# RWKV chain: block inverse of the first half four places later in its slot, group norm of a tile in the next first-half slot

## The chip, the cores and the metric

One NeuronCore of a Trainium2 chip. The metric is the device time of one launch in microseconds (us). Before the change three runs took 3611.99, 3619.16 and 3623.68 us, median 3619.16.

## What is computed

A backbone of four layers over 256 context and 256 latent tokens, width 1024, fp32. Layers 0 and 3 mix tokens with a bidirectional RWKV-7 delta rule, layer 1 with Mamba-2, layer 2 with windowed attention; a gated ConvFFN follows each. The change touches the RWKV mixer alone:

```python
def step(s, inp):                       # one token of one direction, state s (64 x 64) of each of 16 heads
    r_t, w_t, k_t, v_t, kk_t, a_t = inp
    s_kk = einsum('bhvk,bhk->bhv', s, kk_t)
    s = s * w_t - s_kk (kk_t * a_t) + v_t k_t
    return s, einsum('bhvk,bhk->bhv', s, r_t)
...
y = head_groupnorm(ys[0] + ys[1], ln_g, ln_b) + bonus     # bonus: per head, times v
y = (y * (sigmoid(xg @ g1) @ g2)) @ wo
```

## The kernel before

The kernel is written engine by engine: TensorE (PE), VectorE (DVE), ScalarE (ACT), GpSimd (POOL) and SyncE (SP) each run their own program and meet at semaphores. The RWKV mixer first projects (r, k, v and three low-rank inputs), then works through eight tiles of 128 channels (two heads each). A tile has 512 tokens in eight chunks of 64, for each of two directions. Within a chunk the recurrence is written with the inverse of a 64 x 64 triangular matrix; from chunk to chunk it is a chain.

`slot_steps` (L2384) sets one order that all engines follow, each taking the steps it has code for. Seventeen slots, numbered h from 0: slot 2i, an **even slot**, prepares the first half (four chunks) of tile i, slot 2i+1, an **odd slot**, its second half. In each slot the chain runs over four chunks of the half prepared in the slot before. A chain chunk is six places: W, U, S, each for two directions, so a slot has places 0 to 23. The other steps stand in two lists, `early` (ahead of the chain step of that place) and `late` (behind it). A step on an engine waits at its turn, and what stands behind it on that engine waits too. The steps spoken of:

- **W, U, S**: chain. PE multiplies into PSUM; ACT copies W's result (L2835), DVE copies U's (L3194), and S ends with the new state on DVE (L3205), for which ACT scales the old one (L2930). S writes no state in the last chunk of a tile, which is the last of an even slot.
- **GT**: PE forms the matrices to invert, ACT copies them. SP sends them to DRAM and back with another layout (L2499, L2507), POOL inverts 16 x 16 blocks in **IB** (L3003 to L3009), SP sends the result out and back (L2514, L2522), and DVE spreads it in **E** (`expand`: two products L3158, two transposes L3162, L3163). GT of a first half stands at places 0, 1 of an odd slot, GT of a second half at 19, 20. E of a second half is at place 2 of an odd slot.
- **Z, X**: two levels (16, 32) that grow the block inverse to 64: four Z and four X on PE per half, of 16 matmuls each, with copies on ACT (Z) and DVE (X, L3185, and a transpose L3190).
- **H2, HB, R**: products of keys; H2 uses PSUM bank 6, and DVE masks its result (L3177).
- **L01, L23, KS, ...**: staging of tile i+1 in the even slot: low-rank products, two sigmoids each on ACT (L2846), scans on DVE (L3084) with L3088, L3092, L3097 behind, and **ar0**, **ar1**, the last operations, on POOL (L2997, L2998); ar1 follows the last chain step of the even slot.
- **P1, P2, P2e, P2v, P3**: group norm of a finished tile. P2 is a 128x512 matmul of variances into bank 6 on PE, then a logarithm (L2946) on ACT; P2e the exponential (L2950) on ACT; P2v two products on DVE (L3213, L3215); P3 the gate's matmul into bank 6 and on DVE the output of the tile (L3220). They stand at places 18 to 22 of the odd slot after the tile's chain has ended. YE copies a tile's chain output out of PSUM at an even slot's end.

In layer 3 only the latent half of the tokens is wanted behind the chain, so its group norm works on 256 columns in place of 512.

Of the kernel before, what the change touches and what calls it, by code (L numbers as in the profile page):

```python
# [134 lines left out]
def program(nc, a, out, draft, scratch, blocks_dram, layers=range(DEPTH), mixers=True, only=range(DEPTH)):  # L135
    C = Counts(draft)
    ctx = ExitStack()
    with ctx:
# [38 lines left out]
        vec_done = sem("vec_done")  # L177
# [2206 lines left out]
        def slot_steps(h):  # L2384

            i, s = h // 2, h % 2
            chain = [(k, 2 * ((h - 1) // 2) + d, 4 * ((h - 1) % 2) + c) for c in range(4) for k in "WUS" for d in range(2)]
            chain = chain if h else []
            if h == SLOTS:

                steps = []
                for n, step in enumerate(chain):
                    steps.append(step)
                    if n % 2:
                        steps.append(("O", n // 12, n // 2 % 6, n // 2 % 6 + 1))
                return steps + [("YE", i - 1), ("O", 2, 0, 3), ("P1", i - 1), ("O", 2, 3, 6), ("P2", i - 1)] + [
                    ("O", m, 6, 7) for m in range(3)] + [("P2e", i - 1), ("O", 3, 0, 4), ("P2v", i - 1), ("P3", i - 1),
                                                         ("O", 3, 4, 7)]
            both = (2 * i, 2 * i + 1)
            more = i + 1 < KD  # L2400
            levels = [(k, q, s, m) for m in range(len(LEVELS)) for k in "ZX" for q in both]
            early, late = [], []
            if s == 0:
                at = (4, 5, 7, 8, 10, 11, 13, 14) if i else (21, 21, 22, 22, 23, 23, 24, 24)
                early += [(k, *step) for k, step in zip(at, levels)]
                early += [(1 if i else 20, "E", i, 0), (0, "R", i, 0, 0), (2, "R", i, 0, 1), (9, "H2", both[0], 0),
                          (12, "HB", both[0], 0, 0), (15, "HB", both[0], 0, 1), (16, "H2", both[1], 0),
                          (18, "HB", both[1], 0, 0), (20, "HB", both[1], 0, 1)]
                late.append((3, "Rv", i, 0))
                if i == 0:  # L2410
                    early += [(0, "IB0", 0, 0), (0, "IB", 0, 1), (0, "kf", 1), (0, "TS", 1)]
                else:
                    late.append((3, "IB", i, 1))
                if more:
                    late += [(k, n, i + 1) for k, n in (
                        (1, "L01"), (2, "sc0"), (3, "L23"), (3, "sub0"), (3, "sc1"), (4, "TL"), (4, "sub1"),
                        (5, "sum1"), (6, "KS"), (7, "KE"), (8, "pn0"), (9, "pr0"), (9, "pn1"), (11, "rm0"), (12, "ax0"),
                        (13, "ax1"), (14, "ar0"), (15, "ad0"))]
            else:
                at = (5, 6, 8, 9, 12, 13, 15, 16)  # L2420
                early += [(k, *step) for k, step in zip(at, levels)]
                early += [(2, "E", i, 1), (14, "R", i, 1, 0), (17, "R", i, 1, 1), (2, "H2", both[0], 1),
                          (3, "HB", both[0], 1, 0), (4, "HB", both[0], 1, 1), (7, "H2", both[1], 1),
                          (10, "HB", both[1], 1, 0), (11, "HB", both[1], 1, 1)]
                late.append((18, "Rv", i, 1))
                if more:
                    early += [(d, "GT", i + 1, 0, d) for d in range(2)] + [(19 + d, "GT", i + 1, 1, d) for d in range(2)]
                    late += [(1, "ar1", i + 1), (8, "IB", i + 1, 0)]
                    late += [(k, n, i + 1) for k, n in (
                        (3, "pct"), (4, "rm1"), (6, "pr1a"), (7, "ad1"), (8, "pr2a"), (12, "pr1b"), (13, "pr2b"), (14, "bsum"),  # L2430
                        (14, "bs"), (16, "BV"), (16, "BVv"), (19, "sd0"), (19, "sd1"), (13, "VT"))]
                if i + 2 < KD:
                    late += [(23, "kf", i + 2), (23, "TS", i + 2)]
                if i:
                    late += [(k, n, i - 1) for k, n in ((4, "P1"), (18, "P2"), (18, "P2e"), (21, "P2v"), (22, "P3"))]
            steps = []
            for k in range(25):
                steps += [e[1:] for e in early if e[0] == k]
                if k < len(chain):
                    steps.append(chain[k])  # L2440
                steps += [b[1:] for b in late if b[0] == k]
            if s == 0 and i:
                steps.append(("YE", i - 1))
            return steps
# [100 lines left out]
        def rwkv_pe(l, lo):  # L2545
            t = f"r{l}"
# [67 lines left out]
            def grams_k(q, s):  # L2614
                i, d = q // 2, q % 2
                if d:
                    pe.wait_ge(vec_done, C.at(f"{t}.{q - 1}.g2{s}"))
                elif s:
                    pe.wait_ge(vec_done, C.at(f"{t}.{q + 1}.g20"))
                elif i + 1 < KD:  # L2620
                    pe.wait_ge(act_done, C.at(f"{t}.t{i + 1}.kkl"))
                else:
                    pe.wait_ge(vec_done, C.at(f"{t}.t{i - 2}.out"))
                pe.wait_ge(vec_done, C.at(f"{t}.t{i}.sd{d}"))
                ar = AR[i % 2]
                for c in range(4):
                    cs = tok(ORDER_Q[d][4 * s + c])
                    for hs in HALF:
                        if lo and s == 0:
                            last = mm(PS[hs, 6, c * P:c * P + Q], SD[hs, d, cs], ar[hs, d, 0, cs])  # L2630
                        else:
                            last = mm(PS[hs, 6, c * P:c * P + P], SD[hs, d, cs], ar[hs, d, :, cs])
                done(last, f"{q}.h2{s}")
# [106 lines left out]

            def post2(j):
                if j + 2 < KD:
                    pe.wait_ge(vec_done, C.at(f"{t}.t{j + 2}.bv"))
                elif j + 1 < KD:
                    pe.wait_ge(vec_done, C.at(f"{t}.{2 * j + 3}.g21"))
                else:
                    pe.wait_ge(vec_done, C.at(f"{t}.t{j - 1}.out"))
                pe.wait_ge(act_done, C.at(f"{t}.t{j}.sq"))
                done(mm(PS[:, 6, lo:T], const("blkmean"), SQ[:, lo:T]), f"t{j}.va")
# [26 lines left out]
            def l01(n):  # L2776
                if n:
                    pe.wait_ge(act_done, C.at(f"{t}.t{n - 1}.vt"))
                    pe.wait_ge(vec_done, C.at(f"{t}.t{n - 3}.out" if n >= 3 else f"{t}.t{n - 1}.bv"))
                for d in range(2):  # L2780
                    low_rank(n, W2A, TH, d, 6 + d, f"t{n}.pw{d}")

# [611 lines left out]
```

## Time and profile before

| what | value |
|---|---|
| median of three runs | 3619.16 us |
| profiled execution, its own time | 3610.41 us |
| its span | 3608.6 us |
| PE busy over the span | 3447.1 us, 96% |
| DVE, ACT, POOL busy | 69%, 32%, 16% |
| chain, layer 0, 283.8 to 643 us | 359.2 us, PE busy 323.67, granted clock 0.98 |
| chain, layer 3, 2985 to 3342 us | 357.0 us, PE busy 306.68, granted clock 0.98 |

The first rows are of the whole launch, the last two of the stretches in which the seventeen slots run. DVE, ACT and POOL are busy for 222.78, 191.00 and 170.21 us of the first of these. A matmul of 64 columns lasts 218 ns by its record while the next ones follow at a pace of 29 ns, so PE counts as busy in part of a stall.

### The profile page before, as it was taken

The numbers are of one execution on the slowest core, as the hardware profiler recorded it, in microseconds if no ns is written. First come the engines' busy times: TensorE is split into PE (matmuls) and PEld (weight loads), VectorE is DVE, ScalarE is ACT, GpSimd is POOL, SyncE is SP. The second block draws the span as 40 slices with busy tenths as digits, with TensorE's granted clock in tenths as the row PEclk, the third lists the DMA queues.
The fourth block names the chain that finished last, engine by engine and source line by source line (L and its number), as shares of the span: only waits on it lengthen the run. The fifth ranks groups of instructions, "written<-read, shape, count | busy, mean of one in ns | idle before, by whom it ended". The sixth has DMA issues, their size and how long they took to land. (4 is left out here: it accounts for less than half of the span.)

```text
span 3608.6 us, 74335 instructions
## 1 busy us (share of the span) xinstructions
PE 3447.1 (96%) x28653; PEld 2513.5 (70%) x28653; DVE 2487.9 (69%) x4562; ACT 1156.4 (32%) x2482; POOL 590.4 (16%) x1128
## 2 busy tenths in 40 slices
PE   7998998999999999999999999999999997888999
PEld 2447777688786455555888876678877456777887
DVE  7986665489897657653898954469987956664431
ACT  4035554133202444431233014323310225663210
POOL 1015553000000323320000000000000105553000
PEclk9998999999999999999999999999999998999999
DMA  6641111244353323223444520043434541111454
GB/s 219 207 136 24 21 22 32 74 133 130 118 161 97 105 79 102 82 76 99 129 126 127 162 83 28 25 126 121 136 118 129 170 129 25 25 24 27 134 152 133
DMA packets 584315, 365.07 MB, mean 101 GB/s; under 512 B 126144, under 2 KB 553480, under 8 KB 581928
## 3 DMA queue, kind: packets, MB, share of 16 engines
q1 hardware_dynamic: 557544, 250.40, 25.1%
q0 software_dynamic: 26432, 110.07, 8.7%
q8 instruction: 223, 3.65, 0.4%
q14 instruction: 116, 0.95, 0.1%
HBM read 348.73 MB, written 11.67 MB: 100 GB/s over the span
## 5 line engine op out<-in xcount | busy, mean ns | idle before, releaser
L275 PE MATMUL PS<-H,WR 128*128 128x512 f32 (+1 forms) x1424 | 477.1, 494 | 0.0
L591 DVE SCALAR_TENSOR_TENSOR WORK<-WORK,SC 128x512 f32<-128x512 f32 x616 | 418.3, 746 | 0.7
L275 PEld LDWEIGHTS PS<-H,WR 128*128 128x128 f32 x1424 | 268.0, 190 | 187.3 <-issue 167.2
L2549 PE MATMUL PS<-WORK 64*64 64x64 f32 (+2 forms) x6944 | 361.0, 231 | 29.5 <-ACT BIG L2846 16.6
L571 POOL DMA_DIRECT2D WORK<-in_ada_w_dram x88 | 66.4, 755 | 1857.7 <-DVE WORK L591 839.6
L1474 PE MATMUL PS<-BIG,WR 128*128 128x512 f32 (+1 forms) x944 | 329.4, 503 | 5.2 <-DMA WR<-in_rw_wo_dram 1.7
L2549 PEld LDWEIGHTS PS<-WORK 64*64 64x64 f32 (+1 forms) x6944 | 282.1, 139 | 69.2 <-ACT WORK L2835 23.0
L1474 PEld LDWEIGHTS PS<-BIG,WR 128*128 128x128 f32 x944 | 175.7, 190 | 132.6 <-issue 111.8
L2835 ACT ACTIVATE WORK<-PS 128x64 f32<-128x64 f32 (+3 forms) x528 | 161.4, 326 | 292.0 <-PE PS L2549 286.7
L1012 ACT ACTIVATE WORK<-PS 128x512 f32<-128x512 f32 x252 | 134.7, 541 | 335.6 <-PE PS L945 285.1
L945 PE MATMUL PS<-BIG 128*128 128x256 f32 x984 | 223.9, 380 | 0.0
L275 PE MATMUL PS<-WORK,WR 128*128 128x512 f32 (+1 forms) x544 | 211.7, 545 | 0.9 <-DMA WR<-in_rw_wr_dram 0.9
L945 PEld LDWEIGHTS PS<-BIG 128*128 128x128 f32 x984 | 186.0, 190 | 25.1
L2549 PE MATMUL PS<-BIG,WORK 64*64 64x64 f32 x1920 | 145.7, 228 | 47.0 <-DVE WORK L3194 36.3
L945 PE MATMUL PS<-H,BIG 128*128 128x256 f32 x768 | 177.8, 380 | 0.6 <-ACT H L728 0.4
L945 PE MATMUL PS<-BIG,WORK 128*128 128x256 f32 x792 | 176.3, 379 | 0.0
L1093 DVE SCALAR_TENSOR_TENSOR WORK<-WORK,PV 128x510 f32<-128x510 f32 x252 | 171.7, 743 | 2.6 <-ACT WORK L1023 2.6
L275 PEld LDWEIGHTS PS<-WORK,WR 128*128 128x128 f32 x544 | 102.0, 190 | 101.0 <-issue 88.5
L945 PEld LDWEIGHTS PS<-BIG,WORK 128*128 128x128 f32 x792 | 150.5, 190 | 20.5
L945 PEld LDWEIGHTS PS<-H,BIG 128*128 128x128 f32 x768 | 145.2, 190 | 22.5 <-ACT H L728 3.0
L3009 POOL TENSOR_TENSOR BTN<-BTN,BTP 64x14 f32<-64x14 f32 (+1 forms) x420 | 149.8, 357 | 32.9
L2549 PEld LDWEIGHTS PS<-BIG,WORK 64*64 64x64 f32 x1920 | 100.6, 136 | 74.0 <-DVE WORK L3194 23.4
(363 smaller groups left out, 6391.0 us busy)
## 6 DMA issues: line engine op xcount, KB each, us to landing
WORK<-in_ada_w_dram POOLq DMA_DIRECT2D x88, 1024.0 KB, 6.3
WR<-in_ffn_w_in_dram SPq DMA_DIRECT2D x220, 256.0 KB, 2.9
BIG<-in_ffn_w_in_dram SPq DMA_DIRECT2D x132, 256.0 KB, 3.4
WR<-in_ffn_w_out_dram SPq DMA_DIRECT2D x106, 256.0 KB, 2.8
WR<-in_ssd_w_in_dram SPq DMA_DIRECT2D x96, 256.0 KB, 2.8
BIG<-scratch_dram POOLq DMA_DIRECT2D x8, 2048.0 KB, 7.9
BIG<-in_ffn_w_out_dram SPq DMA_DIRECT2D x36, 256.0 KB, 3.2
BIG<-in_ada_w_dram SPq DMA_DIRECT2D x4, 2048.0 KB, 15.5
```

Source lines behind the costliest of these rows:

```text
L275: mm = pe.matmul(outs, WR[:, slot, k, 0:m], rhs(k), start=first and k == 0, stop=last and k == nk - 1)
L571: pool.dma_start(AW[:, 2048 * h:2048 * h + 2048].rearrange("p (k c) -> p k c", k=4), rows(a["ada_w"][l])[:, 4 * h:4 * h + 4, n * 512:n * 5 ...
L591: lag(vec.scalar_tensor_tensor(ACC3[:, s_], w, by, ACC3[:, s_], ALU.mult, ALU.add), label)
L945: mm = pe.matmul(out, lhs(k), rhs(k), start=start and k == 0, stop=stop and k == 3)
L1012: s(act.activation(EV[f % 2][:, n0:n0 + n, :], ps[:, 0:n, :], ACT.Copy), lab(f, "e" + bank))
L1093: lag(vec.scalar_tensor_tensor(dst, whole[h][:, :, t // 2:SEG - 1 + t // 2], tap(t, h, f), dst, ALU.mult, ALU.add), lab(f, "cv") if (t, h) ...
L1474: mm = pe.matmul(PS[:, bank, lo:T], WR[:, opened[label], k, :], rhs(8 * r + k), start=r == 0 and k == 0, stop=last and k == nk - 1)
L2549: return pe.matmul(o, lhs, rhs, start=start, stop=stop)
L2835: s(act.activation(dst, src, ACT.Copy), f"{t}.{label}")
L3009: g(pool.tensor_tensor(below, below, product, ALU.add), f"{t}.t{i}.ib{s_}" if j_ == BLK - 2 else None)
```

## The change

```diff
@@ slot_steps, even slots (s == 0) @@
-                at = (4, 5, 7, 8, 10, 11, 13, 14) if i else (21, 21, 22, 22, 23, 23, 24, 24)
+                at = (8, 9, 11, 12, 14, 15, 17, 18) if i else (21, 21, 22, 22, 23, 23, 24, 24)
                 early += [(k, *step) for k, step in zip(at, levels)]
-                early += [(1 if i else 20, "E", i, 0), (0, "R", i, 0, 0), (2, "R", i, 0, 1), (9, "H2", both[0], 0),
+                early += [(5 if i else 20, "E", i, 0), (0, "R", i, 0, 0), (2, "R", i, 0, 1), (9, "H2", both[0], 0),
...
+                if i >= 2:
+                    late += [(k, n, i - 2) for k, n in ((18, "P2"), (18, "P2e"), (21, "P2v"), (22, "P3"))]
@@ slot_steps, odd slots @@
-                    late += [(k, n, i - 1) for k, n in ((4, "P1"), (18, "P2"), (18, "P2e"), (21, "P2v"), (22, "P3"))]
+                    late.append((4, "P1", i - 1))
+                if not more:
+                    late += [(k, n, i - 1) for k, n in ((18, "P2"), (18, "P2e"), (21, "P2v"), (22, "P3"))]
@@ PE, grams_k (H2): what frees PSUM bank 6 @@
-                    pe.wait_ge(vec_done, C.at(f"{t}.{q + 1}.g20"))
+                    pe.wait_ge(vec_done, C.at(f"{t}.t{i - 2}.out" if i >= 2 else f"{t}.{q + 1}.g20"))
...
-                    pe.wait_ge(vec_done, C.at(f"{t}.t{i - 2}.out"))
+                    pe.wait_ge(vec_done, C.at(f"{t}.t{i}.bv"))
@@ PE, post2 (P2) @@
-                    pe.wait_ge(vec_done, C.at(f"{t}.t{j + 2}.bv"))
+                    pe.wait_ge(vec_done, C.at(f"{t}.{2 * j + 5}.g20"))
@@ PE, l01 (L01) @@
-                    pe.wait_ge(vec_done, C.at(f"{t}.t{n - 3}.out" if n >= 3 else f"{t}.t{n - 1}.bv"))
+                    pe.wait_ge(vec_done, C.at(f"{t}.t{n - 1}.bv"))
```

The levels Z and X and the step E of the first half move four places back in every even slot but the first. P2 to P3 of tiles 0 to 5 move from odd slots 3, 5, ..., 13 to even slots 4, 6, ..., 14; tiles 6 and 7 keep theirs. Nothing is added or left out, and no shape changes. The waits on bank 6 follow the new order.

DVE at the start of an even slot (the names of buffers are those of the profile; L3205 and, changed, L3209 are the new chain state of S; line numbers of the changed kernel are four higher). Before:

```order
L3158 TENSOR_TENSOR WORK<-WORK,K 128x256 x2
L3162 STREAM_TRANSPOSE WORK<-WORK 128x256
L3163 STREAM_TRANSPOSE WORK<-WORK 128x256
L3194 COPY WORK<-PS 128x64
L3084 SCALAR_TENSOR_TENSOR BIG<-WORK,BIG 128x512
L3194 COPY WORK<-PS 128x64
L3170 TENSOR_TENSOR WORK<-PS,K 128x2x256
L3088 TENSOR_TENSOR BIG<-BIG 128x512
L3084 SCALAR_TENSOR_TENSOR BIG<-WORK,BIG 128x512
L3205 SCALAR_TENSOR_TENSOR WORK<-PS,WORK 128x64
L3092 TENSOR_TENSOR BIG<-BIG 128x512
L3205 SCALAR_TENSOR_TENSOR WORK<-PS,WORK 128x64
```

And changed:

```order
L3198 COPY WORK<-PS 128x64
L3088 SCALAR_TENSOR_TENSOR BIG<-WORK,BIG 128x512
L3198 COPY WORK<-PS 128x64
L3174 TENSOR_TENSOR WORK<-PS,K 128x2x256
L3092 TENSOR_TENSOR BIG<-BIG 128x512
L3088 SCALAR_TENSOR_TENSOR BIG<-WORK,BIG 128x512
L3209 SCALAR_TENSOR_TENSOR WORK<-PS,WORK 128x64
L3096 TENSOR_TENSOR BIG<-BIG 128x512
L3162 TENSOR_TENSOR WORK<-WORK,K 128x256 x2
L3166 STREAM_TRANSPOSE WORK<-WORK 128x256
L3167 STREAM_TRANSPOSE WORK<-WORK 128x256
L3209 SCALAR_TENSOR_TENSOR WORK<-PS,WORK 128x64
```

The four instructions of E stood first; now they stand between the two states of the slot's first chain chunk.

PE at the end of an even slot, changed (64x64 and 64x32 rows are HB, W, U and S; 128x512 rows are P2 and P3):

```order
L2553 MATMUL PS<-K,BIG 64x64 x8
L2553 MATMUL PS<-BIG,WORK 64x64 x2
L2553 MATMUL PS<-WORK,H 64x64 x2
L2553 MATMUL PS<-WORK,K 128x512
L2553 MATMUL PS<-BIG,WORK 64x64 x2
L2553 MATMUL PS<-WORK,H 64x64 x2
L2553 MATMUL PS<-K,BIG 64x64 x8
L2553 MATMUL PS<-WORK 64x64 x4
L2553 MATMUL PS<-WORK,BIG 64x64 x2
L2553 MATMUL PS<-WORK 64x64 x2
L2553 MATMUL PS<-H,WORK 64x64 x2
L2553 MATMUL PS<-WORK 128x512
```

Both 128x512 rows are new here; P2 stands between the two W of the last chunk, P3 between its two S.

DVE at the same place, changed, running into the odd slot:

```order
L3198 COPY WORK<-PS 128x64 x2
L3217 TENSOR_TENSOR WORK<-WORK 128x512
L3219 SCALAR_TENSOR_TENSOR WORK<-WORK,PV,BIG 128x512
L3224 SCALAR_TENSOR_TENSOR BIG<-WORK,PV,PS 128x512
L3162 TENSOR_TENSOR WORK<-WORK,K 128x256 x2
L3166 STREAM_TRANSPOSE WORK<-WORK 128x256
L3167 STREAM_TRANSPOSE WORK<-WORK 128x256
L3181 TENSOR_TENSOR WORK<-PS,K 128x512
L3198 COPY WORK<-PS 128x64 x2
```

The rows of P2v and P3 (L3217, L3219, L3224) are new between the last two copies of U and E of the second half.

## Rows read from the trace of the kernel before

**Rows 1.** Stretches: odd slot 9, even slot 10 (start:end, length, then busy us by engine, granted clock, DMA):
```profile
478.40:503.00 24.60, 22.43 (x562) 18.45 (x562) 15.90 (x41) 12.17 (x32) 9.39 (x29) 1.00 0.16 25
503.00:525.50 22.50, 19.99 (x542) 17.90 (x542) 16.07 (x36) 15.60 (x37) 16.14 (x33) 1.00 0.11 21
```
**Rows 2.** Waits of PE, 283 to 605 us, then 2975 to 3345 us (total, times, longest):
```profile
PE PS L2549 <- DVE WORK L3194: 15.6, 20, 1.9
...
PE PS L2549 <- DVE WORK L3194: 24.9, 30, 2.1
```
**Rows 3.** Timeline, PE and DVE where slot 10 becomes slot 11 (start, busy, [idle before <-releaser]):
```profile
522.00 2.09 DVE L3158 TENSOR_TENSOR WORK<-WORK,K 128x256 f32<-128x256 f32 x2 [1.89 <-DMA WORK<-blocks_dram]
525.82 0.33 PE L2549 MATMUL PS<-BIG,WORK 64*64 64x64 f32 x4 [1.67 <-DVE WORK L3194]
```
**Rows 4.** Timeline, SP's issues for tile 5:
```profile
495.41 0.37 SPq L2522 DMA_DIRECT2D WORK<-blocks_dram  x1
497.41 1.26 SPq L2499 DMA_DIRECT2D blocks_dram<-WORK  x2
...
519.61 0.37 SPq L2522 DMA_DIRECT2D WORK<-blocks_dram  x1
```
**Rows 5.** Timeline, POOL at that boundary (ar1):
```profile
521.13 1.27 POOL L2997 TENSOR_TENSOR H<-BIG 128x512 f32<-128x512 f32 x1 [1.35 <-PE PS L2549]
522.49 1.33 POOL L2998 TENSOR_TENSOR H<-BIG,WORK 128x512 f32<-128x512 f32 x1
```
**Rows 6.** Timeline, DVE, step E at the start of slot 13:
```profile
567.79 0.76 DVE L3158 TENSOR_TENSOR WORK<-WORK,K 128x256 f32<-128x256 f32 x2 [0.54 <-PE PS L2549]
568.66 0.45 DVE L3162 STREAM_TRANSPOSE WORK<-WORK 128x256 f32<-128x256 f32 x1
569.03 0.40 DVE L3163 STREAM_TRANSPOSE WORK<-WORK 128x256 f32<-128x256 f32 x1
```
**Rows 7.** Timeline, PE, end of slot 9 (P2, then waits):
```profile
494.02 1.12 PE L2549 MATMUL PS<-WORK,K 128*128 128x512 f32 x2
...
497.10 0.33 PE L2549 MATMUL PS<-WORK 64*64 64x64 f32 x4 [0.52 <-ACT WORK L2835]
...
500.21 0.28 PE L2549 MATMUL PS<-WORK,H 64*64 64x64 f32 x4
500.63 0.33 PE L2549 MATMUL PS<-BIG,WORK 64*64 64x64 f32 x4
```
**Rows 8.** Timeline, ACT, the same place:
```profile
495.25 0.69 ACT L2946 ACTIVATE WORK<-PS,MC 128x512 f32<-128x512 f32 x1 [0.82 <-PE PS L2549]
496.03 0.63 ACT L2950 ACTIVATE WORK<-WORK 128x512 f32<-128x512 f32 x1
```
**Rows 9.** Timeline, PE, end of slot 15 (P2 there has no GT behind it):
```profile
630.93 0.33 PE L2549 MATMUL PS<-WORK 64*64 64x64 f32 x4 [1.18 <-ACT WORK L2835]
```
**Rows 10.** Timeline, PE, start of slot 10 (L23 and a Z; an X; W):
```profile
503.67 1.74 PE L2549 MATMUL PS<-WORK 64*128 64x512 f32 x20 [0.68 <-ACT BIG L2846]
...
508.71 0.66 PE L2549 MATMUL PS<-WORK 64*64 64x32 f32 x16
509.20 0.31 PE L2549 MATMUL PS<-BIG,WORK 64*64 64x64 f32 x4
```
**Rows 11.** Timeline, DVE, the same place:
```profile
506.98 0.25 DVE L3205 SCALAR_TENSOR_TENSOR WORK<-PS,WORK 128x64 f32<-128x64 f32 x1
507.33 0.69 DVE L3092 TENSOR_TENSOR BIG<-BIG 128x512 f32<-128x512 f32 x1
```
**Rows 12.** Timeline, DVE, E of tile 1's first half, layers 0 and 3:
```profile
313.32 0.76 DVE L3158 TENSOR_TENSOR WORK<-WORK,K 128x256 f32<-128x256 f32 x2 [4.73 <-DMA WORK<-blocks_dram]
...
3025.50 0.76 DVE L3158 TENSOR_TENSOR WORK<-WORK,K 128x256 f32<-128x256 f32 x2 [2.99 <-DMA WORK<-blocks_dram]
```
**Rows 13.** Timeline, DVE, E at the start of slot 15, layer 0:
```profile
612.87 0.76 DVE L3158 TENSOR_TENSOR WORK<-WORK,K 128x256 f32<-128x256 f32 x2 [3.98 <-DMA WORK<-blocks_dram]
```
**Rows 14.** Timeline, PE, P2 in layer 3:
```profile
3191.66 0.70 PE L2549 MATMUL PS<-WORK,K 128*128 128x256 f32 x2
```

## The prediction

> **What bounds the kernel now.** The page first: PE is busy for 96% of the launch, and only the two chains, 359 and 357 us, hold stalls that a new order can move. Then the stretches of two slots [rows 1]: an odd slot takes 24.6 us with 22.43 of PE busy, an even one 22.5 with 19.99. PE comes first, with about 2 us of idle time per slot; DVE and ACT have room on the whole (16 us each at most), but they run in order, so what counts is who stands behind whom. Then PE's waits [rows 2]: by far the largest is for the copy of U (L3194), 15.6 us in layer 0 and 24.9 in layer 3. The timeline says where [rows 3]: at the start of the odd slot DVE stands at E of the second half, whose transfer lands at 522.00; PE resumes 3.8 us later, 1.67 us of it idle. So behind PE lies a **round trip**: from the issue of the grams at 497.41 [rows 4], through POOL's block inverse, to E at 522.00, 24.6 us, most of which no engine's order shortens. In layer 0 it begins once GT of the second half is copied (495.41 is the issue before it, so SP had been free since 495.8).
>
> **Part 1: the group norm leaves the odd slot.** P2 fills PE from 494.02 to 495.08 by its successor's start, 1.06 us, and P3 has its shape: 2.1 us. In its wake PE idles 0.52 us for a copy on ACT that stands behind the logarithm and the exponential [rows 7, 8], and 0.3 us at 500.63, where the new state waits behind the norm's products on DVE (500.21 to 500.63 less a pace of 0.12). The odd slot gets 2.9 us shorter. P2 also stands ahead of GT, so the grams could leave some 1.4 us earlier: 1.06 of PE and 0.3 of the queue on ACT; but SP is free only at 495.8, so 1.6 us is the most.
>
> **Part 2: it enters the even slot.** The same 2.1 us of PE, and no longer the delayed state, since the last chunk of a tile writes none. The copy behind logarithm and exponential stays: in slot 15, where no GT fills PE meanwhile, it costs 1.18 us [rows 9]; here the 16 matmuls of an HB fill some 0.47, so I take 0.8, between 0.52 and 1.18. The even slot gets 2.9 us longer. Parts 1 and 2 cancel, 0 per pair of slots, with ends of -0.3 and +0.4.
>
> **Part 3: the levels move back.** An X takes 0.49 us (508.71 to 509.20), and between L23 at 503.67 and the second W at 509.20 PE now does two Z and one X: 1.4 us [rows 10]. That is filler: the chain there waits for the staging's sigmoids on ACT and the scans on DVE. DVE finishes the first new state at 507.23 and the subtraction L3092 at 508.02 [rows 11]; with E behind it (0.76 and two transposes, until 1.64 us after its start [rows 6]) and the state of 0.28, it would finish at 509.9, or 0.5 earlier because L01 no longer stands behind the norm's output. So the W of 509.20 comes at 509.4, although 1.4 us of work has been taken from ahead of it: PE loses about 1.5 us here. Later the levels fill small stalls: the slot has some 0.6 us of them behind the first chunk (22.50 less 19.99 is 2.5 idle, 1.67 of it at E). Net **+0.9 us** per even slot, between 0 (the chain gets by without filler) and +1.6.
>
> **Part 4: where E and the round trip end.** A pair of slots can't go faster than half of round trip plus rest, since the grams of one tile leave before the inverse of the last is used. With 1.6 us less of round trip and 0.9 more of rest, a pair in layer 0 changes by (-1.6 + 0.9)/2, -0.35. Against this stands DVE at the boundary: P3's output, 0.75 us, now stands right ahead of E, so that even a landed inverse is spread only while ar1 runs on POOL from 521.13 to 523.82 [rows 5]. The rows show what that costs: E's two products took 2.09 us at 522.00, of which the second ended only behind ar1, against 0.76 at 567.79, when POOL was quiet [rows 3, 6]. The 1.67 us of idle time would then stay, and come back in the two layer 0 pairs that lack it now (0.54 of waiting at E in slot 13, and PE not idle). I put this between 0 and +1.9 per pair and take +0.8: a pair in layer 0 changes by +0.5, five of them by **+2.5**.
>
> **Part 5: the first tiles, layer 3, the end.** E of tile 1's first half waits 4.73 us in layer 0 and 2.99 in layer 3 [rows 12]. Four places later, about 4 us of PE's work, nearly all of that is covered; but E of its second half is bound by its own round trip, so half of some 3 and 2 us remains, less a starved start: -1 each, **-2**. In layer 3 P2 and P3 take 0.6 us each for 256 columns [rows 14], logarithm and exponential less, E meets ar1 already, and its round trip isn't begun by GT (the issues follow each other), so it doesn't shorten: -0.2 to +0.9 per pair, I take 0. Slot 14, which gets the norm without any staging, has 3.98 us of waiting at E of the last half behind it [rows 13], which cover the 2.9; what slot 13 saves is lost there too.
>
> **Sum.** +2.5 - 2 + 0 = +0.5 us against the profiled execution's 3610.4. That execution lies 8.8 us below the median of the three runs, 3619.2, so the forecast is **3619 us** for the median: no change. A measurement of this kernel can tell about 0.3%, 11 us, from none.
>
> **Rivals.**
> 1. *Covered after all, faster: 3602 us, chance 0.17.* The chain gets through the even slot's start without the filler (part 3 at 0), the 0.8 us of part 2 is covered by the levels that now stand late, and with the shorter round trip E's idle time vanishes: ten pairs gain 1.67 less 0.2 each, 15 us, and tile 1 gives 2. For it: PE has work at all places of an even slot from 2 to 18. Against it: DVE's queue [rows 11].
> 2. *Starved start, slower: 3633 us, chance 0.23.* PE has nothing beside L01, L23 and KS, and the state behind E is late, for 1.6 us in each of the twelve even slots (2 to 12, two layers) that have levels and staging, with nothing given back later: 19 us, less 2 for tile 1 and 3 for the round trip of layer 0. It decides once PE reaches the slot's second W more than 0.9 us ahead of the state. For it: the 0.68 us of idle time ahead of 503.67 [rows 10] is such a wait already. Against it: in layer 3 DVE has no mask of R at that place.
> 3. *The round trip hides everything: 3617 us, chance 0.12.* E lands when it lands; odd slots get shorter and the idle time at E longer by the same amount, and only tile 1's 2 us remain.
> 4. *E beside ar1 in full: 3625 us, chance 0.15.* Part 4 at its upper end: a pair in layer 0 changes by -0.35 + 1.9, five by 7.8, less 2 for tile 1. For it: 2.09 us against 0.76 [rows 3, 6].
> The page "SBUF — State Buffer" of the Trainium skill, section "SBUF: two separate sides", calls the port pair of VectorE and GpSimd an exclusive lock, held for the whole instruction, also against a VectorE operation with two SBUF inputs. By this rule rival 4 comes true wherever E starts beside ar1; the trace agrees so far, with the 2.09 us. I keep it at 0.15 because E may get in ahead of ar1 where the gate is early.
>
> **How the numbers follow.** The forecast has 0.33; with rivals 3 and 4, which no measurement tells from it, "within 0.3%" has 0.60, from 3608 to 3630. Its own ends are -7 (3612: round trip alone, five times -0.8, and 3 for tile 1) and +10 (3629: E beside ar1 in full, 9.5, and +0.5 for five pairs of layer 3, less 2). The range reaches to rivals 1 and 2 less a few us: 3604 to 3634. Faster by over 0.3% has 0.17, slower 0.23.
>
> **What would show it.** PE per odd slot some 2 us less busy and per even slot as much more. Odd slots near 22 us, even ones near 26. At an even slot's start an idle stretch of PE of over 1 us ahead of the first chunk's second W, released by L3209; at its end 0.5 to 1 us for an ACT copy behind L2950. The issue of the second half's grams right behind the load of the first half's inverse, in layer 0 too. E at the odd start beside ar1, with 1.8 us or more for its products. E of tile 1's first half without a wait. I am wrong if PE's idle time for L3198 at odd starts is gone (rival 1), or if even slots take over 27 us (rival 2).

## The result and the profile after

Four executions of the changed kernel took 3640.41 to 3649.97 us, median 3646.53, against 3619.66 for the kernel before: ratio 1.0078, 95% interval 1.0063 to 1.0093. The change makes the launch slower by 28 us by this ratio. The forecast of 3619 us and its range up to 3634 are both missed. The profiled execution took 3640.41 us against 3610.41, 30.0 more. Taken from the first copy of U to the start of the last slot, layer 0's chain takes 361.2 us in place of 347.4 (+13.8) and layer 3's 332.5 in place of 316.2 (+16.3): the whole difference lies in the two chains. One execution of kernel 12 below, 6665.5 us at a mean granted clock of 0.845, is left out of its ratio.

Stretches of slots 9 and 10, bounded as in [rows 1] by the first copy of U, and then of slot 10's four chain chunks (start:end, length, busy us and instructions of PE, PEld, DVE, ACT, POOL, granted clock, DMA share, GB/s):

```profile
484.77:506.88 22.11, 19.85 (x558) 17.64 (x558) 12.33 (x33) 10.89 (x30) 9.24 (x29) 1.00 0.15 25
506.88:534.66 27.78, 22.49 (x547) 18.66 (x546) 20.06 (x42) 16.59 (x39) 15.57 (x33) 1.00 0.11 19
...
506.88:514.86 7.98, 5.09 (x93) 3.33 (x94) 7.16 (x14) 4.96 (x10) 4.52 (x11) 1.00 0.09 9
514.86:520.10 5.24, 5.01 (x157) 4.87 (x152) 3.91 (x10) 3.45 (x9) 4.22 (x14) 1.00 0.03 8
520.10:527.31 7.21, 6.96 (x178) 5.99 (x178) 2.81 (x9) 4.29 (x11) 4.23 (x8) 1.00 0.13 20
527.31:534.66 7.35, 5.44 (x126) 4.48 (x126) 6.19 (x10) 3.89 (x12) 2.61 (x2) 1.00 0.17 38
```

The odd slot fell from 24.60 to 22.11 us, the even one rose from 22.50 to 27.78: a pair is 2.8 us longer. PE was busy 2.6 us less in the one and 2.5 us more in the other, so the work moved as forecast; the rest of the even slot's 5.3 us is waiting. Where it waits stands in PE's waits of layer 0 (283 to 655 us; total, times, longest) and in its timeline in slot 10, of which the rows with an idle time ahead are shown, up to the first of slot 11 (start, busy, [idle before <-releaser]):

```profile
PE PS L2553 <- DVE WORK L3198: 19.8, 22, 1.7
PE PS L2553 <- DVE WORK L3209: 15.3, 14, 1.3
PE PS L2553 <- ACT WORK L2839: 5.4, 7, 1.2
```
```profile
507.56 1.13 PE L2553 MATMUL PS<-WORK 64*128 64x512 f32 x4 [0.68 <-ACT BIG L2850]
511.13 0.33 PE L2553 MATMUL PS<-BIG,WORK 64*64 64x64 f32 x4 [1.12 <-DVE WORK L3209]
513.72 0.33 PE L2553 MATMUL PS<-BIG,WORK 64*64 64x64 f32 x4 [1.09 <-DVE WORK L3209]
520.24 0.68 PE L2553 MATMUL PS<-WORK 64*64 64x64 f32 x16 [0.38 <-DVE WORK L3194]
527.91 0.33 PE L2553 MATMUL PS<-WORK 64*64 64x64 f32 x4 [0.71 <-ACT WORK L2839]
535.02 0.33 PE L2553 MATMUL PS<-BIG,WORK 64*64 64x64 f32 x4 [1.67 <-DVE WORK L3198]
```

Before, PE waited for a new chain state (then L3205) 2.4 us in all of this stretch; now 15.3, of which 13.4 are two waits in each of the six even slots 2 to 12. The other four of these rows answer, in order, to [rows 10] (the wait for the sigmoids, unchanged at 0.68), to nothing in slot 10 before (the transpose), to [rows 7] (the copy behind the exponential, which has moved with the norm) and, at the boundary of the slots, to [rows 3], unchanged at 1.67. This last one is called the **boundary stall** from here on; since the copy of U that ends slot 10 stands behind E on DVE, it shows in the length of the fourth chunk. DVE, POOL and SP at the places that matter:

```profile
510.81 0.26 DVE L3209 SCALAR_TENSOR_TENSOR WORK<-PS,WORK 128x64 f32<-128x64 f32 x1
511.18 0.69 DVE L3096 TENSOR_TENSOR BIG<-BIG 128x512 f32<-128x512 f32 x1
511.78 0.84 DVE L3162 TENSOR_TENSOR WORK<-WORK,K 128x256 f32<-128x256 f32 x2
...
513.42 0.24 DVE L3209 SCALAR_TENSOR_TENSOR WORK<-PS,WORK 128x64 f32<-128x64 f32 x1
...
530.17 0.75 DVE L3224 SCALAR_TENSOR_TENSOR BIG<-WORK,PV,PS 128x512 f32<-128x512 f32 x1
530.83 2.46 DVE L3162 TENSOR_TENSOR WORK<-WORK,K 128x256 f32<-128x256 f32 x2
```
```profile
530.32 1.27 POOL L3001 TENSOR_TENSOR H<-BIG 128x512 f32<-128x512 f32 x1 [5.21 <-PE PS L2553]
531.67 1.33 POOL L3002 TENSOR_TENSOR H<-BIG,WORK 128x512 f32<-128x512 f32 x1
```
```profile
502.08 0.36 SPq L2526 DMA_DIRECT2D WORK<-blocks_dram  x1
502.55 1.26 SPq L2503 DMA_DIRECT2D blocks_dram<-WORK  x2
...
523.83 0.36 SPq L2526 DMA_DIRECT2D WORK<-blocks_dram  x1
531.73 1.26 SPq L2503 DMA_DIRECT2D blocks_dram<-WORK  x2
```

SP shows the round trip in a new light. The second half's grams leave right behind the load of the first half's inverse (0.47 us, against 2.0 in [rows 4]), as forecast. But the load of the inverse is issued at 523.83, 7.0 us ahead of E at 530.83 (in [rows 3, 4] it took 2.4 us to land), and the next grams leave only at 531.73. E no longer waits for a transfer. It waits for DVE, which is busy with the norm's output (L3224), and so starts 0.5 us behind ar1: its two products take 2.46 us against 0.76 in [rows 6].

Two theories for the next step. **A**: the three stalls at an even slot's start (levels and E) and the boundary stall (norm's output ahead of E, ar1 on POOL) are two separate causes that meet. **B**: the stalls simply add up from PE's extra load in the even slot, and ar1 matters little.

### The profile page after: what moved, and what is told of

Same layout as the page of the kernel before. It is cut to its first block and busy times, and to the rows that moved or that the text cites. A ratio compares the mean times of both kernels' runs of the same rounds, so it can differ in the third digit from the quotient of the medians.

```text
span 3638.6 us, 74335 instructions
## 1 busy us (share of the span) xinstructions
PE 3443.3 (95%) x28653; PEld 2511.9 (69%) x28653; DVE 2498.6 (69%) x4562; ACT 1154.7 (32%) x2482; POOL 582.7 (16%) x1128
## 5 line engine op out<-in xcount | busy, mean ns | idle before, releaser
L2839 ACT ACTIVATE WORK<-PS 128x256 f32<-128x256 f32 (+3 forms) x528 | 158.3, 325 | 323.2 <-PE PS L2553 318.4
L945 PEld LDWEIGHTS PS<-H,BIG 128*128 128x128 f32 x768 | 145.2, 190 | 22.5 <-ACT H L728 3.0
L945 PE MATMUL PS<-H,WR 128*128 128x256 f32 x672 | 150.4, 379 | 0.0
## 6 DMA issues: line engine op xcount, KB each, us to landing
BIG<-in_ada_w_dram SPq DMA_DIRECT2D x4, 2048.0 KB, 15.3
```

What stands on the lines that cost most here:

```text
L945: mm = pe.matmul(out, lhs(k), rhs(k), start=start and k == 0, stop=stop and k == 3)
L2839: s(act.activation(dst, src, ACT.Copy), f"{t}.{label}")
```

## Experiments

The ratio is to the kernel before in the same series. Chunk and slot lengths are of slots 9 and 10 of layer 0 in each one's profiled execution, from copy to copy of U; "layer 0" and "layer 3" are the chains as above.

| kernel | ratio [95%] | slot 9 | slot 10: chunks 1, 2, 3, 4 | slot 10 | layer 0 | layer 3 |
|---|---|---|---|---|---|---|
| before | 1 | 24.6 | 8.24, 4.25, 4.28, 5.71 | 22.5 | 347.4 | 316.2 |
| changed | 1.0078 [1.0063, 1.0093] | 22.1 | 7.98, 5.24, 7.21, 7.35 | 27.8 | 361.2 | 332.5 |
| 1 norm only | 1.0013 [1.0000, 1.0025] | 22.1 | 8.19, 4.25, 5.48, 7.35 | 25.3 | 350.0 | 321.6 |
| 2 levels and E only | 1.0033 [1.0024, 1.0043] | 24.6 | 7.98, 5.24, 6.00, 3.96 | 23.2 | 353.5 | 326.0 |
| 3 changed, E early | 1.0068 [1.0051, 1.0085] | 22.1 | 6.83, 5.17, 7.20, 7.34 | 26.5 | 361.0 | 332.1 |
| 4 before, ar1 waits | 0.9976 [0.9967, 0.9986] | 24.6 | 8.25, 4.25, 4.28, 4.60 | 21.4 | 337.1 | 318.9 |
| 5 changed, ar1 waits | 1.0022 [1.0011, 1.0033] | 22.1 | 7.90, 5.15, 7.20, 5.64 | 25.9 | 352.2 | 326.8 |
| 6 norm only, ar1 waits | 1.0026 [1.0015, 1.0038] | 22.1 | 8.17, 4.25, 5.48, 5.65 | 23.6 | 344.1 | 323.3 |
| 7 levels, E, ar1 waits | 1.0019 [1.0009, 1.0029] | 24.6 | 8.13, 5.17, 6.00, 3.96 | 23.3 | 348.4 | 323.6 |
| 8 levels only, E early | 1.0032 [1.0020, 1.0045] | 24.6 | 6.88, 5.36, 6.00, 3.96 | 22.2 | 351.0 | 322.5 |
| 9 as 4, layer 0 alone | 0.9988 [0.9979, 0.9997] | 24.6 | 8.24, 4.25, 4.28, 3.96 | 20.7 | 338.6 | 322.2 |
| 10 changed, norm sooner | 1.0019 [1.0009, 1.0028] | 22.1 | 7.98, 5.24, 8.03, 4.62 | 25.9 | 351.7 | 323.7 |
| 11 levels two places on | 1.0009 [1.0000, 1.0019] | 24.6 | 6.88, 5.39, 5.55, 4.41 | 22.2 | 350.2 | 319.9 |
| 12 norm only, sooner | 1.0020 [1.0009, 1.0031] | 25.4 | 8.18, 4.25, 6.78, 4.62 | 23.8 | 352.0 | 326.8 |

### 1 and 2: the two parts apart

Kernel 1 has all of the diff but the two lines of levels and E; kernel 2 has only those two.

> Only the group norm (P2 to P3) moves to the even slot; levels and E keep their old places. Starved start (the levels that left the even slot's beginning are the cost): the pair of slots pays 2.3 us of TensorE and 0.9 us of the ScalarE queue in the even slot and gets 2.5 us back in the odd one, so 0 to +6 us against before, and the second W of the even slot has no wait for the state. Rival, the norm's place (VectorE's output ahead of E, bank 6) is the cost: +20 to +30 us, as in the full change.

> Only the levels and E move four places back; the group norm stays in the odd slot. Starved start: two idle stretches of about 1.2 us each ahead of the even slot's second chunk, in twelve even slots, of which up to 1.8 us per slot come back where E waits for its transfer at the odd start: +12 to +28 us against before. Rival, the norm's place is the cost: within 3 us of before.

The norm's move costs what the table shows: 2.5 us less in the odd slot, 2.8 more in the even one. The levels' move lengthens the first three chunks by 2.45 us (8.24 + 4.25 + 4.28 to 7.98 + 5.24 + 6.00) and takes 1.75 us off the fourth, since the even slot is now long enough for the inverse to have landed. The two effects don't add: 1.0013 and 1.0033 apart, 1.0078 together. Both kernels came out as their first reading had it (0 to +6 us, and +12 to +28). In kernel 1 and in the full change the fourth chunk ends with the boundary stall (7.35); in kernel 2 it does not (3.96). There both of E's products are done before ar1 starts (POOL 524.41), and take 0.75 us together:

```profile
523.31 0.75 DVE L3158 TENSOR_TENSOR WORK<-WORK,K 128x256 f32<-128x256 f32 x2
```

### 3 and 8: E at its old place

```diff
-                early += [(5 if i else 20, "E", i, 0), ...
+                early += [(1 if i else 20, "E", i, 0), ...
```

In kernel 3 with the rest of the change, in kernel 8 with the levels' new places alone.

> The full change with step E of the first half back at place 1, levels at their new places. If the idle time ahead of the second W comes from E's 1.6 us in VectorE's queue between the two states, that stretch (1.14 us) goes and the run is 12 to 16 us faster than the full change, +12 to +18 against before. If it is the missing filler alone (ScalarE's sigmoids, table load and scale ahead of the state), the stretch stays and the run is within 4 us of the full change, +23 to +30 against before.

> Levels of the first half four places on as in the change, but the spread of the first half stays at place 1 and the norm in the odd slot. Splits the 12 us of the levels alone. If PE lacks work at the even slot's start (no Z and X ahead of the second W) and the spread's place matters little: 3624 to 3630, ratio 1.002 to 1.004. If the cost is the spread's 1.2 us in VectorE's queue ahead of the first new state: the start's stalls go from 3.3 to some 2 us and, where the inverse lands in time, layer 0's even slots from 23.2 to 22: 3614 to 3620, ratio 0.999 to 1.001.

In both, the first chunk shortens by 1.1 us: that is E in DVE's queue ahead of the second new state. The rest of the loss stays. Kernel 8's ratio is where its first reading, the missing filler, had it, though its even slots are as short as the second reading said (22.2 us). Kernel 3 is 3.6 us below the full change by the ratio, within the 4 us of its second reading, though the stretch that this reading wanted unchanged did shrink. The first W of the second chunk still waits (here in kernel 8), and DVE shows why:

```profile
509.90 0.33 PE L2549 MATMUL PS<-BIG,WORK 64*64 64x64 f32 x4 [1.18 <-DVE WORK L3205]
```
```profile
508.41 1.27 DVE L3084 TENSOR_TENSOR_SCAN BIG<-WORK,BIG 128x512 f32<-128x512 f32 x1
509.60 0.25 DVE L3205 SCALAR_TENSOR_TENSOR WORK<-PS,WORK 128x64 f32<-128x64 f32 x1
```

The state has always come behind this scan; PE used to have two Z to do meanwhile. Neither kernel gained as much over the launch as its even slots did: where the inverse of the first half lands late, E early in the queue waits for it, and the copy of U behind E with it. In kernel 3's layer 0, E at the start of slot 2 waits 4.12 us for its transfer, and the last chunks of slots 1, 7 and 13 take 7.4, 7.1 and 5.5 us, where the full change has 4.5, 4.5 and 3.3.

### 4 and 9: ar1 behind the spread

```diff
@@ POOL, rates @@
                 pool.wait_ge(vec_done, C.at(f"{t}.t{n}.kkn"))
+                if s_ and n:
+                    pool.wait_ge(vec_done, C.at(f"{t}.{n - 1}.xi1"))
```

Kernel 9 has `and not lo` behind `n`, so that layer 3 is left as it was.

> The kernel before, with one more wait: GpSimd's ar1 starts only when E of the second half is done. If E's 2.09 us beside ar1 (0.76 alone) is what keeps TensorE idle at the odd start, its idle 1.67 us falls by about 1.3 us in some eleven odd slots: -8 to -14 us against before. If the landing of the transfer alone sets that wait, ar1 costs nothing there and only comes later: 0 to +4 us.

> The kernel before with ar1 behind the spread in layer 0 alone. With the wait in both layers the profiled chain of layer 0 (first U to the last slot's start) was 10.3 us shorter (337.1 against 347.4), that of layer 3 2.7 us longer (318.9 against 316.2): there the transfer lands late, so that ar1 and the first half's grams behind it come late too. If that reading holds: layer 3 as before, layer 0 as with the wait: 10 us less than before, 3605 to 3608, ratio 0.997 to 0.998, and 1 to 3 us below the wait in both layers. Rival: layer 3's 2.7 us lay within what two runs of one kernel differ by (dips of the granted clock): no better than the wait in both, 3608 to 3611.

Kernel 4 is faster than the changed kernel and than the one before: 0.24% less than the latter, 8.7 us by the ratio, as its first reading had it (8 to 14), and 6.2 by the medians (3609.33 against 3615.55). E of the second half at the start of slot 11, and ar1:

```profile
518.47 0.76 DVE L3160 TENSOR_TENSOR WORK<-WORK,K 128x256 f32<-128x256 f32 x2 [2.11 <-DMA WORK<-blocks_dram]
...
521.90 1.73 DVE L3127 TENSOR_TENSOR BIG<-BIG,WORK 128x512 f32<-128x512 f32 x1
```
```profile
520.46 1.27 POOL L2999 TENSOR_TENSOR H<-BIG 128x512 f32<-128x512 f32 x1 [4.42 <-PE PS L2549]
521.81 1.27 POOL L3000 TENSOR_TENSOR H<-BIG,WORK 128x512 f32<-128x512 f32 x1
```

E's products are back at 0.76 us. What stands beside ar1 now is L3127, which takes 1.73 us; in kernel 1 the same instruction, at the same place but behind ar1, takes 0.69. Nobody waits for it. The Trainium skill, page "SBUF — State Buffer", section "SBUF: two separate sides", says that VectorE and GpSimd share a port pair as an exclusive lock, also a VectorE operation with two SBUF inputs against a GpSimd operation that reads SBUF: whichever starts first has it for the whole instruction, and the other is blocked. The trace agrees at both places where VectorE came second: in the change E ended at 533.29, 0.3 us behind ar1's last product (533.00), and here L3127 ended at 523.63, 0.55 us behind it (523.08).

Kernel 9's layer 0 is nearly as short as kernel 4's (338.6, 337.1). Its layer 3 has the code of the kernel before and yet took 322.2 us against 316.2, with a mean granted clock of 0.97 against 0.99. So two executions of the same code can differ by 6 us in layer 3, and the 2.7 us by which I had justified kernel 9 mean nothing. Its ratio of 0.9988 misses the first reading (0.997 to 0.998) and is not better than kernel 4's; its median, 3609.78 us, is where the rival had it.

### 5, 6 and 7: the same wait on the change and its parts

> The full change, and ar1 on GpSimd waits for the spread of the same slot's block inverse, so that the two never lie beside each other. Norm alone cost 5 us, levels alone 12, both together 28 (of 3619): 11 us come from their meeting. Theory A (the norm's output, right ahead of the spread on VectorE, holds it until ar1 has begun, and ar1's lock gives the idle stretch of 1.8 us at the slot's start back in all pairs): the stretch shrinks from 1.83 to some 0.5 us in about 12 pairs, 15 us less than the full change, 3628 to 3633 us, ratio to before 1.003 to 1.005; against the levels alone (1.0033) hardly more. Theory B (the 11 us come from stalls that add up at the even slot's start and end: W 1.3 and 1.1, Z 0.5, copy 0.9): only the 8.7 us that the same wait gave the kernel before, or less: 3637 to 3645, ratio 1.005 to 1.007.

> Norm in the even slot, levels and spread at the old places, ar1 waits for the spread. With the norm alone the idle stretch at an odd slot's start was 2.0 us in nearly all pairs, more often than before. Theory A: about 12 pairs lose 1.4 us of it, 16 us less than norm alone (3621): 3603 to 3608, ratio 0.996 to 0.998, as fast as the kernel before with the same wait (0.9976) or faster, which would make moving the norm worth nothing or a little by itself. Theory B (the norm's place costs its 5 us by the copy behind logarithm and exponential, whatever ar1 does): 3613 to 3616, ratio 0.998 to 1.0.

> Levels and spread of the first half four places on, norm in the odd slot, ar1 waits for the spread. With the levels alone the spread of the second half began ahead of ar1 in most layer-0 pairs already (idle stretch 0.04 us) and stood beside it in about half of layer 3's (1.87). Theory A: only these gain, 5 or 6 pairs by 1.4, 8 us less than levels alone (3628): 3619 to 3622, ratio 1.000 to 1.002, so the levels cost 9 to 12 us against the kernel before with the same wait. Theory B (the wait's gain has nothing to do with where the spread meets ar1): as much as in the kernel before, 8.7 or more, in layer 0 as well. Either way a loss against 3609 says that the levels' move alone is dear.

Kernel 5 comes out as A said, and a little better: the fourth chunk falls from 7.35 to 5.64, and the ratio from 1.0078 to 1.0022. That is 20 us, much more than the 8.7 of kernel 4, which B had as its limit. Kernel 7 gains 5 us against kernel 2, and its ratio is in A's range, but the place is not A's: A spoke of layer 3 alone, and in the profiled executions layer 0's chain is 5.1 us shorter (3.4 of it in slot 14, which has no ar1) and layer 3's 2.4. Kernel 6 fits neither theory: its pair of slots 9 and 10 is down to 45.7 us from 47.3, as A says, but its ratio, 1.0026, is above both ranges and not below kernel 1's (the intervals overlap). Its profiled execution, 3615.8 us, is the shortest of seven, of which five took 3626.7 us or more, so its chain lengths in the table stand for the short ones. Its chunks show waiting elsewhere: the last chunk of odd slots took 7.43 us in slot 7 and 5.77 in slot 13 (layer 0), and 5.9 to 6.3 in slots 5, 7, 9 and 13 of layer 3, where 4.5 or 3.4 would do. That led to kernel 12.

### 10: the same stall removed without touching GpSimd

```diff
-                    late += [(k, n, i - 2) for k, n in ((18, "P2"), (18, "P2e"), (21, "P2v"), (22, "P3"))]
+                    late += [(k, n, i - 2) for k, n in ((17, "P2"), (17, "P2e"), (19, "P2v"), (20, "P3"))]
```

> The full change with the norm of the tile before one place (P2) and two places (P2v, P3) earlier in the even slot, and no wait at ar1. Tests what holds the spread behind ar1's start without touching GpSimd. Theory A (the norm's output, 0.75 us right ahead of the spread on VectorE, does): now the output is done some 1.5 us before the slot ends, the spread starts ahead of ar1 wherever the inverse has landed (all of layer 0), and the 2.0 us of idle time ahead of the next slot's first Z fall to 0.04 in layer 0, in layer 3 in some: last chunk of an even slot 5.5 instead of 7.35 us, 10 to 20 us less than the full change: 3626 to 3636. Against it 0 to 0.7 us per slot for U's copy behind the output. Rival (the spread and ar1 are released together by the same last products, so it meets ar1 whatever stands ahead): chunk still 7.3, 3640 to 3646. The levels alone (idle 0.04) speak for A.

```profile
524.75 0.75 DVE L3224 SCALAR_TENSOR_TENSOR BIG<-WORK,PV,PS 128x512 f32<-128x512 f32 x1
525.41 0.22 DVE L3198 COPY WORK<-PS 128x64 f32<-128x64 f32 x1
525.55 0.75 DVE L3162 TENSOR_TENSOR WORK<-WORK,K 128x256 f32<-128x256 f32 x2
```
```profile
526.43 1.27 POOL L3001 TENSOR_TENSOR H<-BIG 128x512 f32<-128x512 f32 x1 [5.07 <-PE PS L2553]
```

E now starts 0.9 us ahead of ar1 and takes 0.75 us. Chunks 3 and 4 together fall from 14.56 to 12.65 us, 1.9 per even slot. Of this, the 1.67 us at the boundary are gone and 0.45 us for a copy of U behind the norm's output are new; the rest is the copy behind the exponential, which levels and HB now cover (PE's waits for L2839 in layer 0: 1.2 us in all, against 5.4 in the change). Ratio 1.0019, again 20 us less than the change. The median, 3623.05 us, is below A's own range. That the norm's output ahead of E, with ar1 beside it, costs most of the 20 us is now shown by two different edits, one on POOL and one on the order of PE, ACT and DVE.

### 11: the levels two places on

```diff
-                at = (4, 5, 7, 8, 10, 11, 13, 14) if i else (21, 21, 22, 22, 23, 23, 24, 24)
+                at = (6, 7, 9, 10, 12, 13, 15, 16) if i else (21, 21, 22, 22, 23, 23, 24, 24)
```

> The kernel before with the first half's levels two places on instead of four, spread and norm at their old places. With four places (spread early) the first chunk of an even slot had 1.55 us of stalls and the second 0.54, against 0.63 and 0.08. If what counts is that PE has a Z or an X ahead of the second W (filler): with two places one Z of two stands ahead of it and the first X behind, so about half is lost: first two chunks 1.2 to 1.6 us of stalls together, 5 us more than before at most, ratio 0.9995 to 1.0015. If the loss came from the late end of the levels (they block H2 and HB and so the grams, or VectorE's last copies) it grows with the places too, but shows in the third and fourth chunk: 0.3 us or more there.

The first W of slot 10's second chunk, in the kernel before and in kernel 11:

```profile
507.28 0.33 PE L2549 MATMUL PS<-BIG,WORK 64*64 64x64 f32 x4 [0.24 <-DVE WORK L3205]
```
```profile
506.86 0.33 PE L2549 MATMUL PS<-BIG,WORK 64*64 64x64 f32 x4 [0.71 <-DVE WORK L3205]
```

With two Z ahead of it this W waits 0.24 us, with one (kernel 11) 0.71, with none (kernel 8, above) 1.18: each Z taken away adds 0.47 us, which is what a Z takes (505.82 to 506.29 before). The expectation had the place wrong: both Z still stand ahead of the second W, and it is ahead of the first that one is missing. PE's idle time in chunks 1 and 2 together is 0.92 us before, 1.44 in kernel 11 and 2.21 in kernel 8: the dose works as the missing filler says. The other theory may have a part too: in chunk 3 PE idles 0.26 us, before not at all.

### 12: the norm alone, sooner

Kernel 1 with the edit of kernel 10.

> The norm alone moved to the even slot, but one and two places sooner, as in the run before; levels and spread at their old places, no wait at ar1. With the norm alone at the change's places a pair of layer 0 took 47.35 us (25.3 + 22.1), against 47.1 before. Theory A (the norm's own place costs nothing, only its output ahead of the spread does): the even slot's last chunk falls from 7.35 to 4.6 us, the third rises by 0.8, so 23.3 + 22.1 = 45.4 per pair where the inverse has landed, five pairs of layer 0 by 1.7 less than before: 8 us; layer 3 as before or 3 us less: 3604 to 3611, ratio 0.997 to 0.999. Rival (the round trip of the grams through GpSimd is the next bound: with the norm alone and ar1 behind the spread, slots 7 and 13 waited 2.4 to 2.9 us for the transfer though their pair was no shorter than 45.7): what the even slots save comes back as waits for the transfer in odd slots' last chunk: 3614 to 3622, ratio 0.9995 to 1.002.

The fourth chunk is 4.62 us, as A says, and still the kernel is slower than the one before, by 7 us. The rival came out, its ratio at the upper end of its range and its median, 3626.08 us, above it: in layer 0 the last chunks of the odd slots 7, 9 and 13 take 7.4, 7.8 and 6.0 us, where 4.5, 4.5 and 3.3 would do (kernel 10). SP and DVE at the end of slot 9, for the inverse of a first half:

```profile
478.50 1.26 SPq L2503 DMA_DIRECT2D blocks_dram<-WORK  x2
...
501.22 0.37 SPq L2526 DMA_DIRECT2D WORK<-blocks_dram  x1
501.69 1.26 SPq L2503 DMA_DIRECT2D blocks_dram<-WORK  x2
```
```profile
503.50 0.76 DVE L3162 TENSOR_TENSOR WORK<-WORK,K 128x256 f32<-128x256 f32 x2 [4.54 <-DMA WORK<-blocks_dram]
```

From the grams' issue to E pass 25.0 us, and the second half's grams leave right behind the load of the first half's inverse. Where the slots get short, the round trip is the next bound. It isn't even of one length: from the issue to POOL's first instruction it takes 8.3 us here (478.50 to 486.77), and 6.3 at this place in the kernel before (475.47 to 481.81). Why the norm's move alone leaves the launch slower than before with its boundary stall gone, and so why kernels 6 and 12 miss A's ranges, isn't settled; part may be the clock (below).

## Why the prediction was wrong

**What held.** Parts 1 and 2: -2.5 and +2.8 us (kernel 1), where I had -2.9 and +2.9. In part 5, layer 0's first two slots: 2.1 us shorter together, though layer 3's came out 0.5 longer, and layer 0's end (slots 13 to 15) was 2.6 shorter where I had 0. The price of E beside ar1, and the place: [rows 3, 6] had both. Of the signs named for the trace one was off: even slots took 27.8 us, not 26, which I had called the mark of rival 2.

**The step that failed first: part 3's size.** The mechanism, filler that is missed, was right. I took +0.9 us per even slot, with +1.6 as upper end; it is +2.45 (kernel 2). Three sub-steps make nearly all of the 1.55 us. First, I had the state behind E 0.5 us earlier because L01 no longer stood behind the norm's output, and so the second W only 0.2 us later; it came 6.84 us behind the slot's start (513.72), against 6.21 before, and the half microsecond wasn't there. Second, I let the levels fill 0.6 us of small stalls behind the first chunk. There were none to fill: of PE's 2.5 us of idle time in slot 10 before, 0.92 lie in chunk 1 (0.68 of them the wait for the sigmoids), none in chunks 2 and 3, and 1.58 in chunk 4, at the boundary. Third, the levels make a new stall of some 0.4 us at the end of chunk 2, where a Z waits for the transpose of the level before it (520.24). Kernels 8 and 11 say what the 2.45 us consist of: 1.0 us is E between the two states on DVE (chunks 1 to 3 of kernel 8 against kernel 2), 1.5 is the Z and X moved away, most of it filler that used to cover the wait for the scan.

**The step that failed second: part 4's trade.** I credited the shorter round trip with 1.6 us and set E beside ar1 against it with only +0.8 of 1.9. The credit was void: once the even slot is 5 us longer, the chain is the bound, and the inverse has landed some 4.6 us ahead of its use (an estimate, 7.0 less 2.4). With the inverse landed, the boundary stall of [rows 3] should have vanished by itself, as in kernel 2. It stayed in all pairs and came new to the two that lacked it, since the norm's output stood ahead of E. The right reckoning for slots 9 and 10 is +2.45 (levels), +0.3 (norm), 0 (boundary, kept): +2.8, the measured value. Where the boundary stall was absent before, it is 1.75 more: pair 3/4 rose by 4.5 us, and pair 11/12 by 5.7, of which 1.3 lie in slot 12's first two chunks (8.71 and 5.77 us), where the granted clock was at its lower level for 3.4 us. The five pairs of layer 0 give +18.4 us where I had +2.5.

**The step that failed third: layer 3 at 0.** Its five pairs rose by 11.4 us and its end by 4.5. I had taken the absence of a round-trip gain as neutral, and forgot that part 3 applies there as well. Rival 4 came true there too: in all five pairs E's products took 2.8 us beside ar1, and the even slots' last chunks take 6.5 us where they had 5.7 to 6.1. The end is a matter of the round trip: in slot 14 the last grams left 0.4 us behind the slot's start (3309.16), where before they had left 4.9 us ahead of it (3281.05), and PE idled 3.99 us for the copy of U behind E, where before it was 1.49. I had let the waiting at E cover the norm in slot 14, as it did in layer 0. Some of the 16 us is scatter (kernel 9), not all of it.

**The rivals.** Rival 2 (starved start) and rival 4 (E beside ar1 in full) both happened, in the same slots. I priced them as alternatives (and rival 1 counted a stall in ten pairs, two of which had none by part 4). Together they cost more than their sum: kernels 1 and 2 add up to 17 us (0.13% and 0.33%), the change costs 28, and taking away ar1's part alone, by kernel 5 or kernel 10, gives 20 back. The mechanism of both was in the prediction; what it had wrong was part 3's size, and the idea that one risk excludes the other.

## What to carry to other kernels

Work that looks like load on the bound engine may be filler for a wait that is always there: before moving it, ask what the engine would do in its place, and read the wait from the next engine's queue. Two risks in one slot are not alternatives; compute the case where both come true, and when one part of a change makes a stretch longer, recheck every stall that existed because that stretch was short. An operation whose collision costs 1.7 us is cheaper to keep apart, by one wait or by one place in the order, than anything this change tried to balance: keeping it apart was worth 20 us in the change and 9 in the kernel before, though with the norm alone moved (kernels 6 and 12) nothing was gained over the launch.

## What was not expected of the hardware

The granted clock of TensorE also falls inside the chain, behind short waits. In kernel 12 (same columns as above):

```profile
498.00:504.80 6.80, 4.88 (x96) 3.12 (x92) 1.77 (x6) 4.81 (x9) 0.23 (x2) 1.00 0.33 61
504.80:508.20 3.40, 2.92 (x55) 2.95 (x57) 3.30 (x8) 1.77 (x4) 0.59 (x3) 0.51 0.21 19
```

PE had idled for 1.9 of 6.8 us, for the most in a wait of 1.7 us that reaches into the second row (until 505.28), then ran for 3.4 us at the lower level, 1.2 GHz (0.51 of full speed). That the waits bring this about isn't shown: in the changed kernel the six even slots 2 to 12 of layer 0 have the same two waits of about 1.1 us, and in the profiled execution the clock fell in slot 12 alone. Nor does a fall always cost time: kernel 12's first chunk of slot 10 took 8.18 us with the lower level in it, kernel 1's 8.19 us without, while slot 12 of the changed kernel lost 1.3 us. The profiled execution of kernel 3 is at the lower level for 40 us of the two chains as the table has them, that of the changed kernel for 17, that of the kernel before for 14.

Over the launch the clock goes with the scatter: kernel 6's seven executions took 3615.8 and 3616.1 us at a mean granted clock of 0.987 and 0.985, and 3626.7 to 3630.3 at 0.983 and 0.984. Within one kernel, a mean clock lower by 0.001 went with about 2 us (a straight line through all executions, with a level for each kernel). Kernels 3, 6, 8 and 12 have 0.984, 0.984, 0.985 and 0.985 as the mean of their executions, the kernel before 0.9865, so some 2 to 5 us of their times may be clock, by this line; that is an estimate. The 20 us of kernels 5 and 10 don't hang on it: their means, 0.986 and 0.987, stand beside 0.986 for the changed kernel.
